# A two-layer trunk on one core: residual turned unnormalised, rstd applied late, expert rows scaled by GpSimd, last norm shared

## What is computed

```python
# layer 0
z = rms_norm(h, g) @ w_in                    # conv gates and u, q, k, v
h = h + concat([conv_mixer, window_attention]) @ w_out
h = h + swiglu(rms_norm(h, g), gate, up, down)          # width 2816
h = h + sigmoid(rms_norm(h, g) @ w_g) * (p[0] @ w_p)
# layer 1
qkv = rms_norm(h, g) @ w_qkv
h = h + causal_attention @ w_o
h = h + sum over e of gates[:, e] * swiglu_e(rms_norm(h, g))   # top 2 of 8, width 3584
h = h + sigmoid(rms_norm(h, g) @ w_g) * (p[1] @ w_p)
return rms_norm(h, final_norm)
# rms_norm(x, g) = x * rsqrt(mean(x * x) + 1e-6) * g
```

## Time and profile before

| | |
|---|---|
| median of 3 runs | 1488.49 us (1487.6 to 1489.38) |
| profiled execution, its own time | 1487.28 us |
| its span | 1485.5 us |
| mean granted TensorE clock | 0.988 of full |
| TensorE busy | 1433.5 us (97%) |
| VectorE busy | 1151.5 us (78%) |
| ScalarE busy | 950.3 us (64%) |
| GpSimd busy | 73.7 us (5%) |

### The profile page before, as it was taken

The page is one execution under the profiler, slowest core; times in us unless marked ns, Lnnn a source line. Parts: engine busy times, 40 slices in busy tenths (PEclk is TensorE's granted clock), DMA queues, the critical chain, the costliest instruction groups (busy, mean ns, idle before and its releaser), DMA issues.

```text
span 1485.5 us, 20799 instructions
## 1 busy us (share of the span) xinstructions
PE 1433.5 (97%) x7507; PEld 1220.6 (82%) x7507; DVE 1151.5 (78%) x919; ACT 950.3 (64%) x813; POOL 73.7 (5%) x95
## 2 busy tenths in 40 slices
PE   6988999998998999999999999999999999999987
PEld 5978999987997888888888888888888888888765
DVE  5675444466556888888888888888888888888985
ACT  4444434445454777777777777777777777777772
POOL 1000000000000750000000000000000000002000
PEclk9999999999999999999999999999999999999998
DMA  9646755466443799999999999999999999999960
GB/s 326 225 160 232 260 172 195 170 212 193 161 154 116 302 395 393 394 388 373 371 396 381 370 389 385 366 384 386 373 383 384 381 370 394 380 345 399 393 243 29
DMA packets 208705, 457.63 MB, mean 308 GB/s; under 512 B 7385, under 2 KB 49381, under 8 KB 208670
## 3 DMA queue, kind: packets, MB, share of 16 engines
q1 hardware_dynamic: 201184, 429.94, 79.3%
q0 software_dynamic: 5568, 20.52, 3.8%
q10 hardware_dynamic: 1918, 6.69, 1.2%
HBM read 442.42 MB, written 14.70 MB: 308 GB/s over the span
## 4 chain that ended last, share of the span: by engine, by line
PE 90%; DVE 5%; ACT 2%; DMA 1%; issue 1%; ACTq 0%; DVEq 0%; SPq 0%
PE bank L832 62%; PE bank L1166 19%; PE bank L1026 4%; PE bank L1141 2%; DVE w_lo L1227 2%; ACT w_hi L548 1%; PE bank L894 1%; DMA raw<-in_o_exp_down 1%; ACT xn L565 1%; DVE xn L1243 1%; PE bank L1125 0%; PE bank L907 0%; DMA rel<-in_consts 0%; PE bank L932 0%; DVE h L1494 0%
## 5 line engine op out<-in xcount | busy, mean ns | idle before, releaser
L1227 DVE TENSOR_TENSOR w_lo<-raw,w_hi 128x2048 fp32r<-128x2048 f32 x406 | 928.9, 2292 | 248.7 <-ACT w_hi L548 247.8
L548 ACT ACTIVATE w_hi<-raw 128x2048 fp32r<-128x2048 f32 x406 | 778.9, 1919 | 326.9 <-PE bank L832 220.3
L832 PE MATMUL bank<-w_lo,x_hi 128*128 128x512 f32 (+2 forms) x1040 | 404.1, 389 | 2.2 <-DVE w_lo L1227 1.6
L832 PE MATMUL bank<-w_hi,x_hi 128*128 128x512 f32 (+2 forms) x1040 | 397.1, 382 | 0.0
L832 PE MATMUL bank<-w_hi,x_lo 128*128 128x512 f32 (+2 forms) x1040 | 396.4, 381 | 0.0
L832 PEld LDWEIGHTS bank<-w_lo,x_hi 128*128 128x128 f32 x1040 | 195.9, 188 | 42.0 <-DVE w_lo L1227 3.6
L832 PEld LDWEIGHTS bank<-w_hi,x_hi 128*128 128x128 f32 x1040 | 195.7, 188 | 38.5
L832 PEld LDWEIGHTS bank<-w_hi,x_lo 128*128 128x128 f32 x1040 | 196.1, 189 | 35.5
L832 PE MATMUL bank<-x_lo,w_hi 128*128 128x256 f32 x616 | 176.5, 287 | 1.8 <-DVE x_lo L1252 1.8
L1166 PE MATMUL bank<-w_lo,m_hi 128*128 128x512 f32 x448 | 175.3, 391 | 0.3 <-DVE m_lo L1510 0.3
L832 PE MATMUL bank<-x_hi,w_lo 128*128 128x256 f32 x616 | 175.1, 284 | 0.0
(11 more groups left out here) (207 smaller groups left out, 997.4 us busy)
## 6 DMA issues: line engine op xcount, KB each, us to landing
raw<-in_o_exp_gate SPq DMA_DIRECT2D x112, 1024.0 KB, 7.2
raw<-in_o_exp_up SPq DMA_DIRECT2D x112, 1024.0 KB, 7.9
raw<-in_o_exp_down SPq DMA_DIRECT2D x112, 1024.0 KB, 7.6
raw<-in_o_w_qkv SPq DMA_DIRECT2D x12, 1024.0 KB, 5.2
raw<-in_e_ffn_gate SPq DMA_DIRECT2D x11, 1024.0 KB, 5.4
raw<-in_e_ffn_up SPq DMA_DIRECT2D x11, 1024.0 KB, 5.4
raw<-in_e_ffn_down SPq DMA_DIRECT2D x11, 1024.0 KB, 4.9
raw<-in_e_w_in SPq DMA_DIRECT2D x9, 1024.0 KB, 17.4
```

Of the source, the lines that this page charges most:

```text
L548: act.activation(w_hi[:, slot % SPLIT], raw[:, slot], ACT.Copy).then_inc(hi_made, 1)
L832: mm = pe.matmul(dst, stat_hl[a], mov_hl[b], start=start and i == 0, stop=stop and i == 2)
L1227: ve.tensor_tensor(w_lo[:, slot % SPLIT], raw[:, slot], w_hi[:, slot % SPLIT], ALU.subtract).then_inc(lo_made, 1)
```

## The change

1. **Raw residual is turned.** The transposes read `h` (only the first norm still reads `xn`), half of the columns at a time, the first half's ahead of the last bank of the product before. `x_hi` and `x_lo` get the gain when the turned banks are copied: eight pieces of 256 columns each, on ScalarE and VectorE, scaled by a column of `gainT`. `gainT` is made once at the start, from six rows that GpSimd loads, by eight small transposes and a copy.
2. **rstd is applied late.** FFN: VectorE multiplies the gate tile in bank 0 by `rrow` (rstd spread over the partitions by a product with ones) ahead of SiLU, and `add_banks` multiplies by rstd. Gates: the sigmoid's scale. Attention: scores by `q_scale`, k by `rrow` on VectorE, v on ScalarE. The value tile's place moves ahead of the first scores. Router: logits scaled by VectorE.
3. **rsqrt** has fewer dependent steps: the sum is halved first, and each Newton round is two steps instead of three.
4. **Banks** are written and added in the order half 0 of both token halves, then half 1.
5. **Routing.** The comparisons are done for both token halves in one instruction each. Picks come directly from the positions; shares and job lists follow after the first split and the first half of the gathered rows. GpSimd makes the normalised rows `xn` for the experts in four operations of 1024 columns. The projection runs in three pieces: its first half while the ranks are made, two banks ahead of the gather and two after.
6. **Last norm.** GpSimd multiplies each quarter of h by the gain when it is ready; ScalarE scales the first two quarters by rstd, VectorE the other two. The sixth norm's turned first half stands ahead of the last scatter product.

```diff
+            for i in range(6):
+                pool.dma_start(gain_rows[i:i + 1, :], gains[i]).then_inc(gain_rows_loaded, 16)
...
+            load_gain(4)
+            pool.wait_ge(x_lo_made, 2 * KC)
...
+            pool.wait_ge(gain_loaded, 16)
+            pool.wait_ge(rstd_made, 5)
+            for t in range(TT):
+                pool.tensor_scalar(xn[:, t], h[:, t], rstd[:, t:t + 1], None, ALU.mult).then_inc(rows_scaled, 1)
+                pool.wait_ge(rows_scaled, 2 * t + 1)
+                pool.tensor_tensor(xn[:, t], xn[:, t], gain[:, :], ALU.mult).then_inc(rows_scaled, 1)
...
+                for q, (half, t) in enumerate(QUARTERS):
+                    cols = slice(half * HALF, (half + 1) * HALF)
+                    pool.wait_ge(h_ready, 4 * 5 + q + 1)
+                    pool.tensor_tensor(hg[:, t, cols], h[:, t, cols], gain[:, cols], ALU.mult).then_inc(h_weighted, 1)
```

```diff
+            def highs(i, half):
+                for g in range(2 * half, 2 * half + 2):
+                    act.wait_ge(xT_ready, 4 * i + g + 1)
+                    for k in range(2 * g, 2 * g + 2):
+                        act.activation(x_hi[:, k, :], bank[TURN_BANKS[i][g]][:, (k % 2) * SEQ:(k % 2 + 1) * SEQ], ACT.Copy,
+                                       scale=gainT[:, k, i:i + 1]).then_inc(x_hi_made, 1)
...
+            def turn_x(i, half):
+                for g in range(2 * half, 2 * half + 2):
+                    pe.wait_ge(*((h_ready, 4 * (i - 1) + 2 * half + 2) if i else (xn_ready, 2 * half + 2)))
+                    for k in range(2 * g, 2 * g + 2):
+                        for t in range(TT):
+                            at = k % 2 * SEQ + t * P
+                            mm = pe.transpose(bank[TURN_BANKS[i][g]][:, at:at + P], (h if i else xn)[:, t, k * P:(k + 1) * P], ident)
                     mm.then_inc(xT_ready, 1)
...
+                part(0, range(KC // 2), True)
+                turn_x(norm, 1)
+                part(1, range(KC // 2), False)
+                part(0, range(KC // 2, KC), False)
+                part(1, range(KC // 2, KC), False)
...
+                down_tile(OUT0_T + i, MHL, 2 * i, 0, i == 0, i == 3, last=i == 3, chunks=chunks,
+                          before={3: lambda: turn_x(1, 0)} if (i, chunks) == (3, (1,)) else None)
```

```diff
+            def lows(i, halves=(0, 1)):
+                for k in [4 * half + c for half in halves for c in range(4)]:
+                    ve.wait_ge(x_hi_made, KC * i + k // 2 * 2 + 2)
+                    src = bank[TURN_BANKS[i][k // 2]][:, (k % 2) * SEQ:(k % 2 + 1) * SEQ]
+                    ve.scalar_tensor_tensor(out=x_lo[:, k, :], in0=src, scalar=gainT[:, k, i:i + 1], in1=x_hi[:, k, :],
+                                            op0=ALU.mult, op1=ALU.subtract).then_inc(x_lo_made, 1)
...
+            def scaled(n, i):
+                ve.wait_ge(tile_used, n + 1)
+                if not isinstance(i, int):
+                    ve.wait_ge(silu_made, i)
+                ve.tensor_tensor(gated_up.rearrange("p (j t) -> p j t", j=2), bank[0][:, :].rearrange("p (j t) -> p j t", j=2),
+                                 rrow[:, :].unsqueeze(1).broadcast_to((P, 2, SEQ)), ALU.mult).then_inc(scaled_made, 1)
...
             def gather_first():
-                pe.wait_ge(pick_made, 1)
+                pe.wait_ge(pick_made, TT)
+                pe.wait_ge(rows_scaled, 2 * TT)
...
+            proj(1, (0, 1))
             gather_first()
+            proj(1, (2, 3))
+            pe.wait_ge(proj_made, 2)
+            gate_up(0, rows=0)
             pe.wait_ge(proj_made, 4)
-            gate_up(0, rows=0)
```

More of the change, by code:

```diff
@@ L686, in sigmoids @@
             def sigmoids(done, n):
[L688 removed]
+                act.wait_ge(rstd_made, 3 if done == 2 else 6)
+                for b in BANKS:
                     wait_sum(act, done, b, n)
[L690 removed]
+                    act.activation(sig[:, b], bank[4 + b][:, :], ACT.Sigmoid, scale=rstd[:, b // 2:b // 2 + 1]).then_inc(sig_made, 1)
             norm(2, lambda: step(PLE0_T - 1))
@@ new lines, in last_norm @@
+            def last_norm():
+                rsqrt(6)
+                ve.wait_ge(h_weighted, 4)
+                for half, t in QUARTERS[2:]:
+                    at = slice(half * HALF, (half + 1) * HALF)
+                    ve.tensor_scalar(xn[:, t, at], hg[:, t, at], rstd[:, t:t + 1], None, ALU.mult).then_inc(late_out, 1)
+            def add_banks(first, done, n):
+                for half, t in QUARTERS:
+                    wait_sum(ve, done, 2 * t + half, n)
+                    at, src = h[:, t, half * HALF:(half + 1) * HALF], bank[first + 2 * t + half][:, :]
+                    if done == 1:
+                        ins = ve.scalar_tensor_tensor(out=at, in0=src, scalar=rstd[:, t:t + 1], in1=at, op0=ALU.mult, op1=ALU.add)
+                    else:
+                        ins = ve.tensor_tensor(at, at, src, ALU.add)
+                    ins.then_inc(h_ready, 1)
@@ L1416, in _, with scale_k @@
+            lows(2)
+            split(PLE0_T - 1 + SPLIT)
+            rsqrt(2)
+            for i in range(3):
                 split(PLE0_T + i + SPLIT)
             embed(0, lambda b: bank[b][:, :])
-            norm(3)
+            lows(3)
             split(PLE0_T + 3 + SPLIT)
+            rsqrt(3)
+            rstd_diag()
+            link(ve.tensor_scalar(q_scale[:, :], rstd[:, :], MOBA_D ** -0.5, None, ALU.mult))
             split(PLE0_T + 4 + SPLIT)
+            def scale_k(i):
+                pair, part = i // 3, i % 3
+                if part == 1:
+                    ve.wait_ge(tile_used, QKV_T + i + 1)
+                    if i == 1:
+                        ve.wait_ge(rrow_made, 2)
+                    ve.tensor_tensor(k1T[:, 2 * pair:2 * pair + 2], bank[i % 4][:, :].rearrange("p (j t) -> p j t", j=2),
+                                     rrow[:, :].unsqueeze(1).broadcast_to((P, 2, SEQ)), ALU.mult).then_inc(k1_made, 1)
+                split(QKV_T + i + SPLIT)
@@ L1430, in _ @@
             add_banks(0, 3, OUT1_T + 3)
-            norm(4)
-            split(OUT1_T + 2 + SPLIT)
+            lows(4)
+            rsqrt(4)
             ve.wait_ge(logits_ready, 1)
-            link(ve.tensor_copy(logit, bank[4][:, 0:2 * E].rearrange("p (t e) -> p t e", t=TT)))
+            for t in range(TT):
+                ins = ve.tensor_scalar(logit[:, t], bank[5][:, t * E:(t + 1) * E], rstd[:, t:t + 1], None, ALU.mult)
+            link(ins)
             link(ve.tensor_reduce(top, logit, AX, ALU.max))
```

458 lines of the change are left out of this document (274 added, 184 removed).

## The result

The changed kernel takes **1479.49 us** (median of 4 runs, 1477.75 to 1480.67), the kernel before 1488.05 in the same session (1486.83 to 1489.38): ratio 0.9943, 95% interval 0.993 to 0.9955. That is 8.6 us faster; 1478.2 was predicted. The profiled run took 1480.57 with a span of 1478.8, against 1487.28 and 1485.5.

The account below looks back on a forecast made before the run. TensorE, busy 97% of the span, was taken to bound the kernel, so time returns only where it idles or runs at a lower clock. The terms summed to -10.3 us, giving 1478.2 us, range 1470 to 1486.

Parts of the forecast that it names:

- Start: Up to TensorE's first product: gain-row transposes delay the rsqrt, fewer steps win some back; +0.3 us, ends -0.7 and +3.
- Second, fourth and sixth norm: TensorE's idle time before these norms' products shrinks and its clock stays up: -3.6, -5.5 and -4.2 us.
- FFN loop: Each of 11 pairs gains one VectorE product (0.69 us) ahead of SiLU, without delaying TensorE: 0 us.
- Attention order: Fourth norm: value tile first removes the first scores' 0.68 us wait; k scaled by VectorE (0.69 against 0.60) costs nothing.
- Fifth norm and routing: Up to the first expert product: gather at about 483.7, that product at 488.7 against 487.57, +1.5 us.
- the clash: Routing and last norm: VectorE and GpSimd each wait for the whole of the other's instruction; without it, routing -1.5 us.
- Last norm: From the end of the gate: -2.0 us if nothing else comes, +1.9 with VectorE delayed by GpSimd; +1.0 taken.
- The clash case: Last norm: GpSimd's gain products meet VectorE's embedding; last h at +5.7 instead of +2.07 us, giving +1.9.
- The first: Rival, chance 0.25: VectorE and GpSimd exclude each other one-sidedly or rarely; routing -1.5, last norm -2.0, time 1472.2 us.
- The second: Rival, chance 0.12: the second, fourth and sixth norm give only 6.6 us; time 1484.9 us.
- The third: Rival, chance 0.05: the FFN loop's new product joins TensorE's chain, 14.3 us over 11 pairs; time 1492.5 us.

## Why the prediction held

- **Total: right.** 1478.2 against 1479.49, direction and size. Without the window attention's 3.1 us the two traces differ by 9.8, and 10.3 was predicted; part of the closeness is luck, as errors of both signs met (start 1.9 and sixth norm 1.1 better, routing 2.3 and last norm 1.8 worse).
- **Start, +0.3 against -1.6: its middle was too careful.** The gain rows landed in 5.2 to 5.4 us, not up to 10, and the rsqrt began at 11.44 (11.4 worked out). Of the four scalings, estimated at 0.55 each, one took 0.42 (1.67 for four). TensorE's first product came at 18.06 instead of 18.83. The rest, 0.8 by the first conv tile, is put down to the clock by the products' durations (0.28 us, or 0.41): before, the longer ones lay between 20.2 and 23.6, where the granted clock is 0.50 (20.4 to 23.4); after, on seven products until 19.5, although the profile grants 1.00 there. Such a placement isn't safely the change's: the first conv tile began at 41.1 and 41.5 before, and at 39.0 to 40.5 in eight profiles with the changed start.
- **Second, fourth and sixth norm, -13.3 against -14.4: mechanism and size right.** The gaps of 4.5 to 6.1 us became 1.3 to 1.8, and the clock stayed at 1.00. The experiment with the rsqrt in front shows the cause: 12.6 us come back. In the sixth norm, 1.1 better than forecast, the eight transposes ahead of the last scatter product took 1.0 us where the sum left 1.6, and those inside the tile 0.9 instead of 1.4.
- **FFN loop, 0: right.** The product that scales a gate bank takes 0.69 with idle time on either side of it, and the pairs keep their distance. VectorE's timeline and the chain:

```profile
197.03 0.69 DVE L1539 TENSOR_TENSOR work<-bank,rrow 128x512 f32<-128x512 f32 x1 [1.51 <-PE bank L930]
198.98 2.29 DVE L1354 TENSOR_TENSOR w_lo<-raw,w_hi 128x2048 fp32r<-128x2048 f32 x1 [1.25 <-ACT w_hi L566]
```

```profile
191.24 11.51 PE bank L930 x96
202.76 5.47 PE bank L1131 x24
208.22 11.51 PE bank L930 x96
```

- **Attention order: one line of it wrong.** "k scaled by VectorE ... costs nothing" failed: 1.24 us at the second head, as VectorE had its splits first. Against the kernel before, this ate the 0.7 that the order gave at the first head; with the old order, by the experiment on it, the stretch would be 1 us longer still.
- **Fifth norm and routing, +1.5 against +3.9: another wait than forecast, and two terms too small.** The forecast had the clash hold VectorE's chain, so that the gather waited for the picks, 10.2 us after rstd (473.5 to 483.7). In the changed kernel the clash made the picks only 1.3 us later than in the kernel with the rows on VectorE, and TensorE waited for the rows themselves, 11.2 us after rstd. They were late because the forecast took 1.3 us for a GpSimd scaling of 1024 columns, near the memset's 0.97, and it takes 2.9: two of them make 3.2 of the 3.5 us between 7.3 and 10.8. The rest is clock: behind the idle 4.1 us the gather took 5.44 instead of 3.57, at a granted clock of 0.50 from 477 to 479, where the forecast had put 0.4 us. The routing alone took 7.8 us more than before against 5.5 forecast: 1.0 of the difference lies ahead of the gather and 1.3 between it and the first expert product. The other 0.8 of this row is the attention's. With ScalarE scaling, the clash did delay VectorE's chain, as worked out. That it falls on steps with two SBUF operands, by which the forecast counted the held ones here and in the last norm, was the author's assumption, and no run shows it: held were additions with two (0.69 to 1.6 in the last norm) and a step with one (0.17 to 1.87), while four steps with two took their usual 0.28 and 0.29 beside a GpSimd scaling.
- **Last norm, +1.0 against +2.8: a step named and then discounted.** The clash case gave +1.9; the middle was taken "as the queues may interleave better". They didn't: three of the four additions took 1.6 to 1.7. The last h came at 5.1 after the gate, 3.0 later than before but earlier than the 5.7 worked out. What the forecast had wrong behind it is the saving: a shorter rsqrt and the scaling halved onto two engines were to give 2.0 us from the last h to the end, and that stretch took 8.3 us against 8.5. SyncE's timeline, before and after, shows why: from the issue of the first of the four output DMAs to the end it is 4.5 us in both kernels (at 1485.5 and 1478.8), although the last quarter was scaled 3.6 us ahead of the end instead of 2.6. With VectorE alone (the last norm's experiment) it is 4.5 too.

```profile
1480.98 2.32 SPq L405 DMA_DIRECT2D out<-xn  x4
```

```profile
1474.32 1.82 SPq L413 DMA_DIRECT2D out<-xn  x4
```

- **Rivals.** The first (the clash one-sided or rare) fell with the additions of 1.6 us: VectorE is held too. The second, whose 1484.9 sets the upper end of the range, fell: that the three norms give only 6.6 us is shown by no run, they gave 14.4, with gaps of 1.3 to 1.8 and a granted clock of 1.00. The third fell as the FFN loop stayed free.

## What to carry to other kernels

Before a stage's end is shortened by a second engine, ask whether it shares something with the first: here GpSimd's help cost 8.3 us more than VectorE doing it all, though VectorE was already at 78%. Look also at what comes behind the shortened step: scaling the last rows on two engines gained nothing, as the output DMAs set the end (4.5 us from the first one's issue, in each of three kernels). A norm's scale that commutes with the product is worth taking out of the path whole; turned raw but with the rsqrt still in front, it gave nothing (12.6 us slower than with the late rstd). Judge a few microseconds by several traces: one trace put 3.1 us of clock on a stage that the change does not touch.

## What the runs showed of the hardware

- GpSimd at 128 partitions, in the experiment on its prices: a product by a per-partition value of 1024 columns took 2.87 us, dearer than the elementwise product's 2.35; an elementwise product of 512 columns 1.27; a memset of 2048 columns 1.82.
- VectorE was held by GpSimd's instruction and ended 0 to 0.6 us behind it: an addition to h of 0.69 took 1.6 in the last norm, and with ScalarE scaling the rows, 0.29 became 2.34 and 0.17 became 1.87. GpSimd was held as well, 1.27 became 1.6 in the last norm. Not all rows agree. In the changed kernel, VectorE's products of two SBUF operands (128x128, 467.04 to 468.2) took their usual 0.28 and 0.29 beside GpSimd's scaling at 465.98, and the step of 1.87 (line 1634, 128x16) has one tile as operand. Which pairs exclude each other is left open.
- After the attention's idle of 0.8 and 1.3 us the same twelve products took 3.0 us in one execution of the kernel before, at a granted clock of 1.00 (90 to 102), and 4.5 us in another, at 0.86.
